# The second half's mixer: projection blocks in another order, convolution steps spread out, scores from split operands

## The chip, the cores and the metric

The kernel runs on one core of one Trainium2 chip. The metric is the device time of one execution in microseconds (us); lower is better. Engines are named as in the profile: PE (TensorE matmul), PEld (its weight load), DVE (VectorE), ACT (ScalarE), POOL (GpSimd), SP (SyncE, which here only starts the weight transfers).

## What is computed

The reference chains two blocks of two layers each, on 256 positions of width 1024, in float32. The change is in the mixer of the second block, which runs once per layer, so twice. Cut to that mixer:

```python
u = rms_norm_2(h, norm_mix[i])
q, k, v, c, g = jnp.split(u @ w_in[i], splits, axis=-1)      # 512, 128, 128, 1024, 2048 columns
q = rms_norm_2(q.reshape(B, S, N_HEADS, HEAD_DIM), q_norm[i])      # 8 heads of 64
k = rms_norm_2(k.reshape(B, S, KV_HEADS, HEAD_DIM), k_norm[i])     # 2 heads of 64
y_attn = window_attention(q, k, v, sink[i], rel_bias) @ w_attn_out[i]   # scores, bias, sink, softmax
c_val, c_gate = jnp.split(c, 2, axis=-1)
c = c_val * jax.nn.sigmoid(c_gate)
c = depthwise_conv(c, conv_w[i], conv_b[i])                  # 31 taps, 512 channels
c = jax.nn.silu(layer_norm_2(c, conv_ln_g[i], conv_ln_b[i]))
y_conv = c @ w_conv_out[i]
g_attn, g_conv = jnp.split(jax.nn.sigmoid(g), 2, axis=-1)
h = h + (g_attn * y_attn + g_conv * y_conv) @ w_o[i]
```

## The kernel before, in words

**Weights.** All weight matrices are one stream of blocks of 128x2048 floats. SP's queue brings block n into one of four slots of `raw` once PE has finished block n-4 (`blk_done`). ACT copies it, rounded, to `whi` (`split_hi`, L472), and DVE writes the rest, raw minus whi, to `wlo` (`split_lo`, L1094). Both do so two blocks ahead of PE (`AHEAD = 2`). PE then forms each product in float32 accuracy from three one-pass matmuls on rounded parts: hi by hi, hi by lo, lo by hi (`mm3`, L1973). A block of two 128x256 outputs is 48 matmuls.

**Every engine runs its own program in written order** and meets the others only at semaphores. Nothing is reordered at run time; what stands ahead of an instruction on its engine delays it. A DVE `split_lo(n)` waits for ACT's `split_hi(n)`, and PE's block n waits for `split_lo(n)`.

**The mixer (`window(l)` on ACT, DVE and PE).** It takes 16 such blocks, G to G+15: three for queries and keys (`sc` 16 to 21), one for values (`t_block`, evacuated by ACT), then the convolution's value and gate blocks in turn (four: value to `prod`, gate to `gated`, ACT's Sigmoid, product to `cpad`), then eight blocks of gates g. Blocks alternate between two PSUM banks of `ab`; `scaled_evac` (L1504, DVE) empties one with the factor of the RMS norm. `step()` is `split_lo(g+2)` and on to the next block.

**Norm of queries and keys.** ACT squares the six tiles (L941); PE sums them over the heads (`wvar_ps`, six matmuls in full float32, L2496); ACT takes Ln (L958) and Exp (L963), which gives `wstd_ready`; DVE scales the six tiles (L1814), which gives `wqk_ready`. PE's first scores wait for that.

**Attention.** `attend(i)` does three stages for three heads: scores of head i (L2371: one float32 matmul over the head's 64 rows, and two one-pass matmuls that add the position bias from `hank`; all of it twice, for two blocks of 128 queries), transposes of head i-1 (L2380, after `p_norm`, the normalised weights from ACT L827), and the product with the values of head i-2 (L2399, after `pt_ready`). DVE takes the maximum (`top`, L1651, L1655), ACT the Exp (L836), DVE the reciprocal of the sum (`normal`). PE runs one block G+5 to G+14 ahead of each of attend(0) to attend(9). Block G+15 follows attend(9).

**Convolution.** 31 taps on four channel groups of 128x256 are 124 DVE instructions per layer (L1780 for the first tap, L1784 for the rest), which `TAP_PLAN` spreads over ten steps, 12 or 14 instructions each. At the end DVE adds the four groups (L1794, L1795: `conv_ready`), PE takes the mean (L2514), and the convolution's layer norm follows; PE meanwhile does the first block of the attention's output projection, and waits in its middle for the variance (L2519).

Of the kernel before, what the change touches and what calls it, by code (L numbers as in the profile page):

```python
# [18 lines left out]
F32 = mybir.dt.float32  # L19
# [7 lines left out]
P = 128  # L27
# [65 lines left out]
def build(nc, xT, xn, lnrows, gaterows, stream, start, mods, params, wbd, wa2, pT, pos, masks, onehot, rb, toep, outT):  # L93
    with ExitStack() as ctx:
# [360 lines left out]
        def _(act):  # L455
# [473 lines left out]
            def window(l):  # L929
# [5 lines left out]
                for _ in range(3):  # L935
                    split_hi(g[0] + AHEAD)
                    tick()

                split_hi(g[0] + AHEAD)
                act.wait_ge(bank_evac[(a[0] - 1) % 2], (a[0] - 1) // 2 + 1)  # L940
                nc.scalar.activation(sc[:, 32:38, :], sc[:, 16:22, :], ACT.Square).then_inc(wsq_ready, 1)  # L941
                act.wait_ge(rcol_ps, l + 1)
                nc.scalar.activation(small[:, 8:10], mb[:, 0, 0:2], ACT.Copy).then_inc(rcol_ready, 1)
# [6 lines left out]
                tick()  # L950

                for j in range(12):
                    split_hi(g[0] + AHEAD)
                    if j == 0:
                        act.wait_ge(wvar_ps, l + 1)
                        for i in range(3):
                            bank = [mb[:, 0, :], mb[:, 1, :], acc[:, 0, :]][i]
                            ins = nc.scalar.activation(sc[:, 32 + 2 * i:34 + 2 * i, :], v2(bank), ACT.Ln,  # L958
                                                       bias=col("eps6"))
                        ins.then_inc(wln_ready, 1)  # L960
                        act.wait_ge(wln_ready, l + 1)

                        nc.scalar.activation(sc[:, 32:38, :], sc[:, 32:38, :], ACT.Exp, scale=-0.5)\  # L963
                            .then_inc(wstd_ready, 1)
                    elif j in (1, 3):
                        act.wait_ge(bank_evac[a[0] % 2], a[0] // 2 + 1)
                        nc.scalar.activation(gated, gated, ACT.Sigmoid).then_inc(csig_ready, 1)
                    tick()
                    if j >= 1:
                        attend(8 + 8 * l, j - 1, 1.0, l)  # L970
# [1758 lines left out]
```

## Time and profile before

| | |
|---|---|
| time, median of 3 runs | 2356.0 us (2355.74 to 2357.81) |
| the profiled execution's own time | 2353.87 us |
| its span, first to last instruction | 2352.1 us |
| PE busy | 2242.0 us, 95% |
| DVE busy | 1765.5 us, 75% |
| ACT busy | 1192.8 us, 51% |
| mean granted TensorE clock | 0.992 of full speed |
| share of the chain that ended last, by engine | PE 78%, DVE 12%, ACT 5%, DMA 3%, issue 2% |

The two mixers' 16 blocks stand at 1354 to 1484 us and at 1947 to 2080 us of the span. The rows further down are from the timeline (start, duration, engine, line, operation, written<-read, count, and in brackets the idle time of the engine before it and who ended it) and from a table of stretches.

### The profile page before, as it was taken

What the parts mean: (1) busy time and instruction counts of PE and PEld (TensorE: products, weight loads), DVE (VectorE), ACT (ScalarE), POOL (GpSimd) and SP (SyncE); (2) the same over time, 40 slices, a digit from 0 to 9 for tenths busy, and PEclk for the clock granted to TensorE, in tenths of its full rate; (3) what the DMA queues carried; (4) which work ended last, traced back from release to release, by engine and by line L of the source; (5) the groups of instructions that cost most, each with busy time, mean ns of one, the idle gap of its engine ahead of it and who ended that gap; (6) DMA issues with size and microseconds to landing.
All of it is one profiled execution on the core that took longest, in us unless ns stands there. A gap on an engine that the chain in (4) does not pass through costs nothing.

```text
span 2352.1 us, 36839 instructions
## 1 busy us (share of the span) xinstructions
PE 2242.0 (95%) x14676; PEld 2026.0 (86%) x14676; DVE 1765.5 (75%) x1857; ACT 1192.8 (51%) x1297; POOL 237.0 (10%) x199
## 2 busy tenths in 40 slices
PE   4999889999999998999999999999999999999999
PEld 4998789788889877788788998988998899798899
DVE  5898786788789985867667569877567746997755
ACT  2444555455455445555455455655455535565544
POOL 0113000001101300000022000012002200001200
PEclk9999999999999999999999999999999999999999
DMA  8996433567669852455555443445545554245553
GB/s 347 346 361 243 168 131 126 206 251 283 247 233 359 315 212 83 176 190 215 187 179 186 171 161 108 162 180 191 183 167 179 191 183 162 93 157 181 187 188 130
DMA packets 75934, 471.48 MB, mean 200 GB/s; under 512 B 8707, under 2 KB 8963, under 8 KB 27580
## 3 DMA queue, kind: packets, MB, share of 16 engines
q1 hardware_dynamic: 53136, 383.80, 44.7%
q0 software_dynamic: 18976, 68.71, 7.8%
q10 hardware_dynamic: 3724, 17.56, 2.0%
q8 instruction: 74, 1.21, 0.2%
q14 instruction: 24, 0.20, 0.0%
HBM read 468.97 MB, written 1.06 MB: 200 GB/s over the span
## 4 chain that ended last, share of the span: by engine, by line
PE 78%; DVE 12%; ACT 5%; DMA 3%; issue 2%; ACTq 0%; DVEq 0%; SPq 0%
PE ab L1973 18%; PE acc L1973 13%; PE acc L2114 12%; PE mb L2006 10%; PE ab L2006 9%; PE mb L2008 5%; PE ab L2008 5%; DVE wlo L1094 3%; ACT whi L472 2%; PE mb L2371 1%; DMA modmem<-mods 1%; DMA par<-params 1%; DMA raw<-stream 1%; DVE sc L1784 1%; DVE sc L1233 1%
## 5 line engine op out<-in xcount | busy, mean ns | idle before, releaser
L1094 DVE TENSOR_TENSOR wlo<-raw,whi 128x2048 fp32r<-128x2048 f32 x361 | 831.8, 2307 | 247.7 <-ACT whi L472 245.0
L472 ACT ACTIVATE whi<-raw 128x2048 fp32r<-128x2048 f32 x361 | 689.2, 1911 | 395.9 <-DMA raw<-stream 272.5
L1973 PE MATMUL ab<-uu,whi 128*128 128x256 f32 x3104 | 575.3, 288 | 20.4 <-DVE wlo L1094 9.3
L1973 PEld LDWEIGHTS ab<-uu,whi 128*128 128x128 f32 x3104 | 491.7, 195 | 32.0 <-issue 17.2
L1973 PE MATMUL ab<-uu,wlo 128*128 128x256 f32 x1552 | 443.2, 286 | 0.0
L2006 PE MATMUL ab<-uu,whi 128*128 128x512 f32 x1056 | 377.0, 400 | 8.4 <-DVE uu L1445 5.4
L2006 PE MATMUL mb<-uu,whi 128*128 128x512 f32 x1056 | 377.7, 400 | 3.2 <-DVE wlo L1094 1.8
L1973 PEld LDWEIGHTS ab<-uu,wlo 128*128 128x128 f32 x1552 | 302.1, 195 | 0.0
L1973 PE MATMUL acc<-h_hi,whi 128*128 128x256 f32 (+1 forms) x1032 | 293.7, 285 | 6.6 <-DVE h_lo L1721 2.6
L2008 PE MATMUL ab<-uu,wlo 128*128 128x256 f32 x1056 | 296.8, 281 | 0.0
L2008 PE MATMUL mb<-uu,wlo 128*128 128x256 f32 x1056 | 296.7, 281 | 0.0
L1973 PE MATMUL acc<-h_lo,whi 128*128 128x256 f32 (+1 forms) x1032 | 292.3, 283 | 0.0
L1973 PE MATMUL acc<-h_hi,wlo 128*128 128x256 f32 (+1 forms) x1032 | 292.3, 283 | 0.0
L2006 PEld LDWEIGHTS ab<-uu,whi 128*128 128x128 f32 x1056 | 199.1, 189 | 59.1 <-issue 8.6
L2006 PEld LDWEIGHTS mb<-uu,whi 128*128 128x128 f32 x1056 | 199.1, 189 | 54.7 <-DVE wlo L1094 3.3
L446 POOL TENSOR_TENSOR sc<-sc,rstd 128x512 f32<-128x512 f32 x44 | 120.0, 2727 | 964.4 <-ACT sc L691 964.4
L1973 PEld LDWEIGHTS acc<-h_hi,whi 128*128 128x128 f32 x1032 | 198.1, 192 | 8.4 <-DVE h_lo L1721 3.0
L2008 PEld LDWEIGHTS mb<-uu,wlo 128*128 128x128 f32 x1056 | 200.2, 190 | 0.1
L2008 PEld LDWEIGHTS ab<-uu,wlo 128*128 128x128 f32 x1056 | 200.2, 190 | 0.0
L1973 PEld LDWEIGHTS acc<-h_lo,whi 128*128 128x128 f32 x1032 | 198.2, 192 | 0.1
L1973 PEld LDWEIGHTS acc<-h_hi,wlo 128*128 128x128 f32 x1032 | 198.2, 192 | 0.0
L427 POOL DMA_DIRECT2D modmem<-mods x128 | 68.2, 533 | 947.4 <-DVE sc L1230 668.4
(352 smaller groups left out, 2817.1 us busy)
## 6 DMA issues: line engine op xcount, KB each, us to landing
raw<-stream SPq DMA_DIRECT2D x365, 1024.0 KB, 4.8
modmem<-mods POOLq DMA_DIRECT2D x128, 512.0 KB, 6.0
sc<-lnrows ACTq DMA_DIRECT2D x5, 1024.0 KB, 4.9
sc<-start ACTq DMA_DIRECT2D x4, 1024.0 KB, 16.5
gateb<-gaterows ACTq DMA_DIRECT2D x6, 512.0 KB, 3.7
hank<-toep POOLq DMA_DIRECT2D x8, 192.0 KB, 4.2
x<-xT ACTq DMA_DIRECT2D x1, 1024.0 KB, 31.4
x<-xn ACTq DMA_DIRECT2D x1, 1024.0 KB, 5.0
```

The lines of the kernel that those rows point to most:

```text
L427: pool.dma_start(modmem[:, i % MODRING, :], mods[i]).then_inc(mod_in[i % MODRING], 16)
L446: nc.gpsimd.tensor_tensor(gated, gated, r, ALU.mult).then_inc(g2_ready, 1)
L472: nc.scalar.activation(whi[:, n % RAW, :], raw[:, n % RAW, :], ACT.Copy).then_inc(hi_ready, 1)
L1094: nc.vector.tensor_tensor(wlo[:, n % RAW, :], raw[:, n % RAW, :], whi[:, n % RAW, :].bitcast(F32), ALU.subtract).then_inc(lo_ready, 1)
L1233: nc.vector.scalar_tensor_tensor(out=out, in0=part, scalar=cact[:, k:k + 1], in1=out, op0=ALU.mult, op1=ALU.add).then_inc(mod_done, 1)
L1784: ins = nc.vector.scalar_tensor_tensor(out=sc[:, 28 + c, :], in0=cpad[:, c, t:t + T], scalar=w, in1=sc[:, 28 + c, :], op0=ALU.mult, op1=AL ...
L1973: ins = nc.tensor.matmul(out, l, r, start=first and i == 0, stop=last and i == 2, skip_group_check=True)
L2006: nc.tensor.matmul(bank[:, m, :].rearrange("p (a t) -> p a t", a=2), wh[:, k, m * P:m * P + P], uu[:, :, k, :], start=k == 0, stop=k == DM ...
L2008: ins = nc.tensor.matmul(bank[:, m, 0:T], wl[:, k, m * P:m * P + P], u_hi[:, k, :], start=False, stop=k == DM - 1, skip_group_check=True)
L2114: ins = nc.tensor.matmul(acc[:, 2 * t + c, :], l, w[:, k, 512 * c:512 * c + 512], start=first and k == 0 and w is wh and l is hh, stop=las ...
L2371: ins = nc.tensor.matmul(mb[:, k % 2, o:o + w], l, r, start=(c == 0), stop=(c == len(terms) - 1), skip_group_check=True)
```

## The change

What it does, on ACT, DVE and PE alike:

- **Order of the 16 blocks.** Before: q, q, k, values, conv value 0, conv gate 0, conv value 1, conv gate 1, then eight gates. Now: conv value 0, conv gate 0, q, q, k, conv value 1, conv gate 1, values, then eight gates. `lay_out` writes the stream in the new order.
- **Attention's places.** attend(0) now follows block G+6 and attend(1) follows the values' block G+7; attend(2) to attend(9) follow G+8 to G+15. So attend(9) follows the last block, where before it stood one block ahead.
- **The sums of squares** (`variances`) stand between the two halves of block G+5, the second conv value block; before, they followed a whole conv value block.
- **Scores.** The one float32 matmul becomes three one-pass matmuls on rounded parts. So ACT writes the scaled queries' and keys' rounded part to `h_hi` (four instructions per layer, in two groups), and DVE the rest to `h_lo` (four instructions per layer, in two groups, between its scaling instructions). attend(0) waits for the first group, attend(2) for the second.
- **Taps** are spread over 15 steps, beginning after block G+1. The counts are pairs of instructions: 2, 3, 3, 2, 3, 2, 4, 5, 7, 6, 6, 6, 6, 4, 3.

```diff
+TAP_PLAN = {1: (0, 0, 2), 2: (0, 2, 3), 3: (0, 5, 3), 4: (0, 8, 2), 5: (0, 10, 3), 6: (0, 13, 2), 7: (0, 15, 4),
...
@@ ACT, window
+                act.wait_ge(bank_evac[a[0] % 2], a[0] // 2 + 1)
+                nc.scalar.activation(sc[:, 32:38, :], sc[:, 16:22, :], ACT.Square).then_inc(wsq_ready, 1)
+                tick()
+
+                act.wait_ge(wvar_ps, l + 1)
...
+                act.wait_ge(wln_ready, l + 1)
+                nc.scalar.activation(sc[:, 32:38, :], sc[:, 32:38, :], ACT.Exp, scale=-0.5).then_inc(wstd_ready, 1)
+                split_hi(g[0] + AHEAD)
+                act.wait_ge(cn_ready, 2 + 2 * l + 1)
+                for i in (0, 4):
+                    ins = nc.scalar.activation(h_hi[:, 16 + i, :], sc[:, 16 + i, :], ACT.Copy)
+                ins.then_inc(cnhi_ready, 1)
...
@@ DVE, window
+                scaled_evac(prod)
+                step()
+                taps(*TAP_PLAN[5])
+                link(nc.vector.tensor_scalar(small[:, 0:1], col("q_norm_2", l), 64.0 ** -0.5, None, ALU.mult))
+                dve.wait_ge(wstd_ready, l + 1)
+                scale_qk((0, 4)).then_inc(cn_ready, 1)
+                scale_qk((1, 2))
+                dve.wait_ge(cnhi_ready, 2 + 2 * l + 1)
+                rest_qk(((0, 1), (4, 1))).then_inc(wqk_ready, 1)
+                scale_qk((3, 5)).then_inc(cn_ready, 1)
+                scaled_evac(gated)
+                dve.wait_ge(cnhi_ready, 2 + 2 * l + 2)
+                rest_qk(((1, 3), (5, 1))).then_inc(wqk_ready, 1)
+                step()
+                top(n, 0, 1.0, l)
+                conv_in(2)
+                taps(*TAP_PLAN[6])
+                normal(n, 0, l)
+                step()
...
@@ PE, window
+                a_block(g[0], a[0], None, (0, 1), variances)
+                g[0] += 1
+                a[0] += 1
+                a_static(1)
...
-                    return [(sc[r, 16 + h // 2, qb * P:qb * P + P], sc[r, 20 + h // 4, :], 0, T),
+                    qs, ks = slice(qb * P, qb * P + P), 20 + h // 4
+                    return [(h_hi[r, 16 + h // 2, qs], h_hi[r, ks, :], 0, T),
+                            (h_lo[r, 16 + h // 2, qs], h_hi[r, ks, :], 0, T),
+                            (h_hi[r, 16 + h // 2, qs], h_lo[r, ks, :], 0, T),
                             (flip[:], hank_hi[:, h, P * (1 - qb):P * (1 - qb) + T], 0, T),
...
+                pe.wait_ge(wqk_ready, 2 + 2 * l + 1)
+                pe.wait_ge(hanklo_ready, 1)
+                attend(8 + 8 * l, 0, qk, lambda h, kt: vw[:, kt, 64 * (h // 4):64 * (h // 4) + 64], l)
+                v_an = a[0]
+                t_block(P)
+                attend(8 + 8 * l, 1, qk, lambda h, kt: vw[:, kt, 64 * (h // 4):64 * (h // 4) + 64], l)
```

**Place 1, ACT, around the norm of queries and keys.** The rows name line, operation, written<-read and the semaphores waited for; line numbers of the changed kernel differ. Before:

```order
L472 ACTIVATE whi<-raw 128x2048 [waits raw_ready2]
L958 ACT_TABLE_LOAD
L958 ACTIVATE sc<-mb,par 128x512 [waits wvar_ps]
L958 ACTIVATE sc<-mb,par 128x512
L958 ACTIVATE sc<-acc,par 128x512
L963 ACT_TABLE_LOAD
L963 ACTIVATE sc<-sc 128x1536 [waits wln_ready]
L472 ACTIVATE whi<-raw 128x2048 [waits raw_ready3]
L967 ACT_TABLE_LOAD
L967 ACTIVATE sc<-sc 128x512 [waits bank_evac1]
```

Now:

```order
L470 ACTIVATE whi<-raw 128x2048 [waits raw_ready2]
L948 ACTIVATE small<-mb 128x2 [waits rcol_ps]
L950 ACTIVATE sc<-sc 128x1536 [waits bank_evac0]
L956 ACT_TABLE_LOAD
L956 ACTIVATE sc<-mb,par 128x512 [waits wvar_ps]
L956 ACTIVATE sc<-mb,par 128x512
L956 ACTIVATE sc<-acc,par 128x512
L959 ACT_TABLE_LOAD
L959 ACTIVATE sc<-sc 128x1536 [waits wln_ready]
L470 ACTIVATE whi<-raw 128x2048 [waits raw_ready3]
L963 ACTIVATE h_hi<-sc 128x256 [waits cn_ready]
L963 ACTIVATE h_hi<-sc 128x256
```

The weight copy behind the Exp is that of block G+7 before and now. What moved is the copy of block G+6, which now stands ahead of the Square (first row), and the first group of ACT's new copies to `h_hi`, which stands behind the copy of G+7.

**Place 2, DVE, from the evacuation ahead of the scaling to the one behind it.** Before (block G+4's evacuation, the lo part of G+6, the scaling):

```order
L1504 TENSOR_TENSOR sc<-ab,rstd 128x512 [waits blk_done]
L1094 TENSOR_TENSOR wlo_49<-raw,whi 128x2048 [waits hi_ready]
L1811 TENSOR_SCALAR small<-par 128x1 [waits wstd_ready]
L1814 SCALAR_TENSOR_TENSOR sc<-sc,small 128x256 [waits dve_chain]
L1814 SCALAR_TENSOR_TENSOR sc<-sc,small 128x256 x3
L1814 SCALAR_TENSOR_TENSOR sc<-sc,par 128x256 x2
L1504 TENSOR_TENSOR sc<-ab,rstd 128x512 [waits blk_done]
L1094 TENSOR_TENSOR wlo_49<-raw,whi 128x2048 [waits hi_ready]
L1819 TENSOR_TENSOR sc<-sc 128x2x256 [waits csig_ready]
```

Now (block G+5's evacuation, the lo part of G+7, six tap instructions, the scaling, and block G+6's evacuation):

```order
L1523 TENSOR_TENSOR sc<-ab,rstd 128x512 [waits blk_done]
L1113 TENSOR_TENSOR wlo_49<-raw,whi 128x2048 [waits hi_ready]
L1801 SCALAR_TENSOR_TENSOR sc<-sc,par 128x256 [waits tap_done] x6
L1838 TENSOR_SCALAR small<-par 128x1
L1816 SCALAR_TENSOR_TENSOR sc<-sc,small 128x256 [waits wstd_ready,dve_chain]
L1816 SCALAR_TENSOR_TENSOR sc<-sc,par 128x256
L1816 SCALAR_TENSOR_TENSOR sc<-sc,small 128x256 x2
L1823 TENSOR_TENSOR h_lo<-sc,h_hi 128x256 [waits cnhi_ready]
L1823 TENSOR_TENSOR h_lo<-sc,h_hi 128x256
L1816 SCALAR_TENSOR_TENSOR sc<-sc,small 128x256
L1816 SCALAR_TENSOR_TENSOR sc<-sc,par 128x256
L1523 TENSOR_TENSOR sc<-ab,rstd 128x512 [waits blk_done]
```

Before, the lo part of G+7 stood behind the scaling; now it stands ahead of it, and waits for `hi_ready` of block G+7. Six tap instructions stand ahead of the scaling too; between the scaling instructions stand the new subtractions to `h_lo`.

**Place 3, the mixer's end.** DVE before:

```order
L1784 SCALAR_TENSOR_TENSOR sc<-sc,par 128x256 [waits tap_done] x6
L1686 TENSOR_TENSOR h_lo<-acc,h_hi 128x256 [waits ohi_ready]
L1794 TENSOR_TENSOR sc<-sc 128x512 [waits tap_done]
L1795 TENSOR_TENSOR sc<-sc 128x256 [waits dve_chain]
L1094 TENSOR_TENSOR wlo_49<-raw,whi 128x2048 [waits hi_ready]
L1504 TENSOR_TENSOR sc<-ab,rstd 128x512 [waits blk_done]
L1834 SCALAR_TENSOR_TENSOR sc<-mb,sc 128x1024 [waits cmean_ps]
```

DVE now:

```order
L1801 SCALAR_TENSOR_TENSOR sc<-sc,par 128x256 [waits tap_done] x14
L1705 TENSOR_TENSOR h_lo<-acc,h_hi 128x256 [waits ohi_ready]
L1872 TENSOR_TENSOR sc<-sc 128x512 [waits tap_done]
L1873 TENSOR_TENSOR sc<-sc 128x256 [waits dve_chain]
L1113 TENSOR_TENSOR wlo_49<-raw,whi 128x2048 [waits hi_ready]
L1523 TENSOR_TENSOR sc<-ab,rstd 128x512 [waits blk_done]
L1881 SCALAR_TENSOR_TENSOR sc<-mb,sc 128x1024 [waits cmean_ps]
```

PE before, the last matmuls of block G+15 and what follows:

```order
L1973 MATMUL ab<-uu,whi 128x256 x2
L1973 MATMUL ab<-uu,wlo_49 128x256
L1973 MATMUL ab<-uu,whi 128x256 x2
L1973 MATMUL ab<-uu,wlo_49 128x256
L2514 MATMUL mb<-sc,mean_r_53 128x256 [waits conv_ready]
L1973 MATMUL acc<-h_hi,whi 128x256 [waits lo_ready,olo_ready]
```

PE now:

```order
L2020 MATMUL ab<-uu,whi 128x256 x2
L2020 MATMUL ab<-uu,wlo_49 128x256
L2448 MATMUL acc<-sc 64x256 [waits olo_ready,pt_ready]
L2448 MATMUL acc<-sc 64x256
L2579 MATMUL mb<-sc,mean_r_53 128x256 [waits conv_ready]
L2020 MATMUL acc<-h_hi,whi 128x256 [waits lo_ready,olo_ready]
```

On DVE the rows are the same but for the number of taps; on PE the product with the last head's values (attend(9)) now stands between the last block and the mean, where the whole block G+15 stood between them before.

## Rows read from the trace of the kernel before

**Rows 1.** The page: the chain that ended last, by engine, shares of the span.

```profile
PE 78%; DVE 12%; ACT 5%; DMA 3%; issue 2%; ACTq 0%; DVEq 0%; SPq 0%
```

**Rows 2.** Timeline of PE, one steady step of the first mixer.

```profile
1416.52 0.51 PE L1973 MATMUL ab<-uu,whi 128*128 128x256 f32 x2
...
1422.47 0.70 PE L2371 MATMUL mb<-sc 64*128 64x256 f32 x2
1423.09 0.38 PE L2371 MATMUL mb<-hank_hi,flip 128*128 128x256 f32 x1
...
1424.49 0.60 PE L2380 MATMUL acc<-par,sc 128*128 128x128 f32 x4
...
1426.03 0.51 PE L1973 MATMUL ab<-uu,whi 128*128 128x256 f32 x2
```

**Rows 3.** Timeline of PE, the first mixer from the values' block to head 0's transposes.

```profile
1372.43 0.30 PE L1973 MATMUL ab<-whi,uu 128*128 128x128 f32 x1
...
1383.63 0.81 PE L2496 MATMUL mb<-sc,par 128*128 128x256 f32 x3
...
1386.03 0.58 PE L1973 MATMUL ab<-uu,whi 128*128 128x256 f32 x2
...
1393.81 0.70 PE L2371 MATMUL mb<-sc 64*128 64x256 f32 x2 [1.68 <-DVE sc L1814]
...
1403.16 0.70 PE L2371 MATMUL mb<-sc 64*128 64x256 f32 x2
...
1414.93 0.55 PE L2380 MATMUL acc<-par,sc 128*128 128x128 f32 x3 [1.29 <-ACT sc L827]
```

**Rows 4.** Timeline of PE, the second mixer.

```profile
1986.73 0.48 PE L2371 MATMUL mb<-sc 64*128 64x256 f32 x1 [1.68 <-DVE sc L1814]
...
2007.51 0.90 PE L2380 MATMUL acc<-par,sc 128*128 128x128 f32 x3 [2.43 <-ACT sc L827]
...
2017.76 0.48 PE L2371 MATMUL mb<-sc 64*128 64x256 f32 x1
```

**Rows 5.** Stretches: from:to, length, busy time by engine, clock, DMA.

```profile
1397.00:1399.00 2.00, 2.00 (x11) 2.00 (x11) 1.93 (x6) 0.82 (x3) 0.00 (x0) 0.50 0.00 0
2010.40:2012.00 1.60, 1.60 (x8) 1.55 (x8) 1.60 (x5) 1.60 (x5) 0.00 (x0) 0.50 0.00 0
```

**Rows 6.** Timeline of ACT, the first mixer.

```profile
1386.42 1.27 ACT L958 ACTIVATE sc<-mb,par 128x512 f32<-128x512 f32 x2 [4.61 <-PE acc L2496]
...
1389.58 1.49 ACT L963 ACTIVATE sc<-sc 128x1536 f32<-128x1536 f32 x1
1390.97 1.90 ACT L472 ACTIVATE whi<-raw 128x2048 fp32r<-128x2048 f32 x1
...
1417.24 0.47 ACT L836 ACTIVATE sc<-mb,small 128x256 f32<-128x256 f32 x1 [1.06 <-DVE small L1655]
...
1420.62 0.90 ACT L827 ACTIVATE sc<-sc,small 128x256 f32<-128x256 f32 x2
...
1478.49 0.39 ACT L859 ACTIVATE h_hi<-acc 128x256 fp32r<-128x256 f32 x1 [2.32 <-PE acc L2399]
```

**Rows 7.** Timeline of DVE, a steady step and the mixer's end.

```profile
1423.52 2.29 DVE L1094 TENSOR_TENSOR wlo<-raw,whi 128x2048 fp32r<-128x2048 f32 x1
1425.72 0.69 DVE L1651 TENSOR_REDUCE small<-mb 128x2 f32<-128x512 f32 x1
...
1426.58 2.46 DVE L1784 SCALAR_TENSOR_TENSOR sc<-sc,par 128x256 f32<-128x256 f32 x6
...
1433.31 2.29 DVE L1094 TENSOR_TENSOR wlo<-raw,whi 128x2048 fp32r<-128x2048 f32 x1
...
1482.66 0.42 DVE L1686 TENSOR_TENSOR h_lo<-acc,h_hi 128x256 fp32r<-128x256 f32 x1
```

**Rows 8.** Timeline of PE, the end of the first mixer.

```profile
1477.38 0.86 PE L2399 MATMUL acc<-sc 128*64 128x256 f32 x3
...
1484.23 0.45 PE L2514 MATMUL mb<-sc,mean_r 128*128 128x256 f32 x1
```

More of the change, by code:

```diff
@@ L933, in tick, with sigmoid @@
                     g[0] += 1
-                for _ in range(3):
+                def sigmoid(i):
+                    act.wait_ge(bank_evac[a[0] % 2], a[0] // 2 + 1)
+                    nc.scalar.activation(gated, gated, ACT.Sigmoid).then_inc(csig_ready, 1)
+                split_hi(g[0] + AHEAD)
+                tick()
+                split_hi(g[0] + AHEAD)
+                sigmoid(0)
+                tick()
+                for _ in range(2):
                     split_hi(g[0] + AHEAD)
@@ L950, in window @@
                 tick()
-                for j in range(12):
+                attend(8 + 8 * l, 1, 1.0, l)
+                for i in range(2, 10):
                     split_hi(g[0] + AHEAD)
[L954 to L967, printed above, removed]
                     tick()
-                    if j >= 1:
-                        attend(8 + 8 * l, j - 1, 1.0, l)
-                    if j == 9:
-                        b = a[0] - 3
+                    attend(8 + 8 * l, i, 1.0, l)
+                    if i == 8:
+                        b = a[0] - 4
                         act.wait_ge(bank_evac[b % 2], b // 2 + 1)
@@ L1763, in window @@
             def window(l):
-                for i in range(3):
-                    scaled_evac(sc[:, 16 + 2 * i:18 + 2 * i, :])
-                    step()
+                scaled_evac(prod)
                 step()
@@ new lines, in window @@
+                scaled_evac(gated)
+                dve.wait_ge(cnhi_ready, 2 + 2 * l + 2)
+                rest_qk(((1, 3), (5, 1))).then_inc(wqk_ready, 1)
+                step()
+                top(n, 0, 1.0, l)
+                conv_in(2)
+                taps(*TAP_PLAN[6])
+                normal(n, 0, l)
+                step()
+                top(n, 1, 1.0, l)
+                taps(*TAP_PLAN[7])
+                normal(n, 1, l)
+                for i in range(2, 10):
+                    if i < 9:
+                        scaled_evac(sc[:, 2 * (i - 2):2 * (i - 2) + 2, :])
+                        step()
+                    pair, first, count = TAP_PLAN[6 + i]
+                    if i < 8:
+                        top(n, i, 1.0, l)
+                        taps(pair, first, count // 2)
+                        normal(n, i, l)
+                        taps(pair, first + count // 2, count - count // 2)
+                    else:
+                        taps(pair, first, count)
+                    rest(n, i - 2, l)
+                    if i == 9:
@@ L1978, in split_ready, with a_block @@
                 pe.wait_ge(lo_ready, at(n + 1, it))
-            def a_block(n, an, it=None, ms=(0, 1)):
+            def a_block(n, an, it=None, ms=(0, 1), between=None):
                 split_ready(n, it)
@@ L1987, in a_block @@
                 for m in ms:
+                    if between is not None and m == 1:
+                        between()
                     for k in range(DM):
```

111 lines of the change are left out of this document (56 added, 55 removed).

## The prediction

> **What bounds the kernel now.** I read the chain that ended last first: PE holds 78% of it, DVE 12%, ACT 5% [rows 1]. So work that leaves DVE or ACT gains nothing by itself; what counts is PE's own time and the moments at which PE stands still. Then I walked PE's timeline through the two mixers. A steady step of attention (block, scores, transposes, values' product) repeats every 9.51 us, from 1416.52 to 1426.03, with no idle time in brackets [rows 2]: block 5.95, scores 2.02 (1422.47 to 1424.49), the rest 1.54. DVE's step in that place, from one weight split to the next, is 9.79 us with fourteen tap instructions [rows 7], so PE and DVE are nearly even, and PE is the one that never waits.
>
> PE stands still at two places per mixer ahead of that. In the first mixer it waits 1.68 us for the scaled queries and keys and 1.29 us for the first head's normalised weights [rows 3]; in the second 1.68 and 2.43 us [rows 4]. And the clock falls behind some waits: in the first mixer, scores plus block take 9.35 us (1393.81 to 1403.16) [rows 3] where the steady ones take 7.97 [rows 2], a loss of 1.38; the granted clock is 0.50, the 1.2 GHz level, from 1397 to 1399 [rows 5]. In the second, transposes to the next scores take 10.25 us (2007.51 to 2017.76) [rows 4] against 7.49 (1424.49 to 1431.98, one 9.51 step later than 1422.47) [rows 2], a loss of 2.76 at 0.50 again [rows 5]. All this together is what the change could remove: 1.68 + 1.38 + 1.29 = 4.35 in the first, 1.68 + 2.43 + 2.76 = 6.87 in the second, **11.2 us**.
>
> **One-pass scores.** Removed are 32 float32 matmuls (8 heads, 2 query blocks, 2 layers), added are 96 one-pass ones. The float32 one holds PE for 0.62 us until the bias matmul (1422.47 to 1423.09) [rows 2]. The six float32 matmuls of the sums of squares, over all 128 rows, take 2.40 us, 0.40 each (1383.63 to 1386.03) [rows 3]. The difference of about 0.2 is a pause between the 64-row and the 128-row matmuls, not the passes. A one-pass matmul costs 0.12 (48 of them and a start in 5.95) [rows 2], so three cost 0.36. If the pause stays: 0.62 - (0.36 + 0.2) = 0.06 or 0.07 each, times 32, **2.2 us gained**. I take that, since the new matmuls are 64-row ones as well. Ends: if the pause belonged to float32 and goes, 0.26 each, 8.4 us gained; if each of the three cost 0.22 instead, like the spacing of a lone matmul after a pause, 0.66 against 0.62, some 1 us lost.
>
> The Trainium skill, TensorEngine Tiling (Array Packing), Key Properties, says that a change of tiling mode, not only of tile, drains TensorE. By that rule the pause stays and the gain is 2.2 us; without it, 8.4. The 0.2 us seen here agree with it.
>
> **The wait ahead of attend(0), followed instruction by instruction.** Let zero be the start of the six sums of squares. PE is then free for the scores after 2.40 of sums, the second half of block G+5 (2.9), and block G+6 (5.85): at 11.2. Does the Square come in time? It has half a block, 2.9 us, for an evacuation and the Square; I cost that at nothing, with about half a us to spare.
>
> ACT: Ln starts at 2.79 (1386.42 less 1383.63), Exp at 5.95, and the weight copy of G+7 runs from 7.34 to 9.24 [rows 3, 6]. Before, DVE scaled right behind the Exp. Now DVE has first to write the lo part of G+7, which needs that very copy; so DVE, idle since it emptied block G+5, starts it at 9.3 and takes 2.2 (1423.52 to 1425.72) [rows 7]: 11.5. Six tap instructions, 2.4 [rows 7]: 13.9. The small factor and two scaling instructions, 1.05 at 0.4 each like a tap: 14.95. ACT's two copies of 128x256, 0.39 each [rows 6], overlapping: 15.65. DVE's two subtractions at 0.42 and some overlap (the h_lo row) [rows 7]: 16.4. PE resumes at 16.4 instead of 11.2: **a wait of 5.2 us**, in place of 1.68. Queued behind it on PE are all scores, and behind the split on DVE the evacuation of G+6, which nobody misses for two blocks.
>
> **The wait ahead of the first transposes.** After 16.4 DVE does two scalings, waits for ACT's 128x768 and 128x256 copies, evacuates, subtracts (to 19.7, by the same per-element times), then needs ACT's copy of G+8 (to 20.2), splits (22.4) and takes the maximum (0.86) [rows 7]: 23.3, with ACT's Sigmoid beside it. From the Exp of a head to the end of the next normalisation ACT needs 4.28 (1417.24 to 1420.62 and 0.90) [rows 6], here with the values' evacuation in place of the transposes' copy: 27.6. PE is there after scores 1.95, values' block 5.35 (1372.43 to 1383.63 less a block of 5.85) [rows 3] and scores 1.95: 25.7. **A wait of 1.9 us** if the clock holds. It won't: it fell for a wait of 2.43 and for one of the two of 1.68, so I expect it for 5.2. Then PE loses up to 2.76 as in the second mixer and arrives at 28.5, past 27.6, so the two don't add: 5.2 + 2.8 = **8.0 us** for both waits and the clock, against 7.1 at full clock.
>
> **The mixer's end.** Before, block G+15 hid head 7's last steps: product at 1477.38, mean at 1484.23 with no wait [rows 8]. Now the mean comes right behind the product. ACT's rounded part starts 1.11 us after the product (1478.49 less 1477.38) [rows 6, 8] and takes 0.39; DVE's lo part and the two additions of the taps lead to the mean 1.57 us after the lo part's start (1482.66 to 1484.23) [rows 7, 8]. So the mean starts 3.1 after the product, which itself needs 1.0: **2.1 us of new wait**. The wait for the variance that follows has the same chain as before and stays. 2.1 lies between the waits that did and didn't lower the clock; the variance wait would swallow half of a drop of 2.8, so I add half of 1.4, 0.7.
>
> **The steady steps.** PE's step goes from 9.51 to 9.37. DVE's is 9.79 with fourteen tap instructions; with twelve, 9.0 [rows 7]. One step has fourteen still, and DVE enters the row with 2 to 3 us in hand, so DVE doesn't bind. The taps moved into the first steps run while DVE idled; I cost them at nothing but for the six ahead of the scaling, counted above. The eight new instructions on ACT and DVE, about 2 us on each per layer, are hidden but for those in the chain. The new stream order moves no transfer to another time.
>
> **Sum.** Removed: 11.2 + 2.2 = 13.4. Added per mixer: 8.0 + 2.1 + 0.7 = 10.8, twice 21.6. Net **+8.2 us**. On the profiled execution's own 2353.87 that is 2362.1; that execution lies 2.1 below the median of the runs, 2356.0, so the median comes to **2364 us**, 0.35% slower. A measurement of this kernel can tell about 0.2%, 4.7 us, from no change.
>
> **Rivals.**
> - *The scaling isn't late.* If DVE got the lo part of G+7 without waiting for ACT (scaling ends with the Exp's chain at 13.3 instead of 16.4), the first wait is 2.1 and the clock mostly holds: per mixer 2.1 + 1.9 + 2.1 = 6.1, twice 12.2, less 13.4: 2355 us, no change. If even that wait vanished (everything done by 11.2), 2 x (1.9 + 2.1) = 8.0 less 13.4: **2350.6 us, faster**. It decides from a scaling chain that ends by 11.2. Against it stand the order of DVE's and ACT's instructions and the 9.24 at which the copy ends; for it only that my zero may be off.
> - *The pause was float32's.* The scores gain 8.4, the net is +2.0: 2358 us, the same. PE's step would fall to 9.0, where DVE's 9.0 begins to bind, so little more can come of it. Against: the pause is as long ahead of the bias matmul as 64 against 128 rows would make it.
> - *The clock stays low longer* after 5.2 us than after 2.43, or falls at the end as well: up to 2 us more per mixer, 2368 us.
> - *The change doesn't spread DVE's work*: with DVE binding in the steps of six taps, 9.8 against 9.37 for five steps, 2 us per mixer more: 2368 us as well.
>
> **Chances.** Forecast with its clock variants, slower by over 0.2%: 0.60 (2364, of which 0.15 for the two rivals at 2368). The same: 0.26 (2355 to 2360: half-late scaling 0.13, cheaper pause 0.13). Faster: 0.14, the scaling in time. The range reaches from 2354 to 2369: it leaves out the 2350.6 and a little above the clock's worst, and takes in the scores' ends.
>
> **What would show it.** In the trace after: a wait of about 5 us of PE at the first scores of each mixer, ended by DVE's h_lo; the clock at 0.50 behind it; DVE idle for 3 us ahead of the lo part of G+7, ended by ACT's copy; a wait of 2.1 us at the mean; score groups of 1.9 us and steps of 9.4. Score groups of 1.5 us would refute the pause, and a first wait under 2 us the whole forecast.

## Result, and the profile of the changed kernel

The changed kernel takes 2368.32 us, the median of four runs (2366.73 to 2371.21), the kernel before 2355.87 in four runs on the same chip (2353.01 to 2357.81): 1.0063 times as long, 95% interval 1.0046 to 1.0080. The profiled execution took 2367.62 us with a span of 2365.7, against 2353.87 and 2352.1 before.

The chain that ended last, by engine, answers [rows 1]: PE's share rose from 78 to 82%.

```profile
PE 82%; DVE 9%; ACT 5%; DMA 2%; issue 1%; ACTq 0%; DVEq 0%; SPq 0%
```

PE's timeline at the first mixer answers [rows 3] and [rows 2]. Columns: start, busy us, engine, line, operation, written<-read, shapes, count, and in brackets the idle time ahead and what ended it. First the sums of squares, then each place's first row.

```profile
1386.64 1.89 PE L2547 MATMUL mb<-sc,par 128*128 128x256 f32 x8
...
1403.16 0.58 PE L2420 MATMUL mb<-h_hi 64*128 64x256 f32 x1 [5.14 <-DVE h_lo L1823]
...
1406.35 0.31 PE L2020 MATMUL ab<-whi,uu 128*128 128x128 f32 x1
...
1416.61 0.58 PE L2420 MATMUL mb<-h_hi 64*128 64x256 f32 x1
...
1420.51 0.78 PE L2020 MATMUL ab<-uu,whi 128*128 128x256 f32 x2
...
1427.49 0.38 PE L2420 MATMUL mb<-h_hi 64*128 64x256 f32 x1
...
1429.37 0.60 PE L2429 MATMUL acc<-par,sc 128*128 128x128 f32 x4
...
1430.90 0.39 PE L2020 MATMUL ab<-uu,whi 128*128 128x256 f32 x1
...
1436.85 0.38 PE L2420 MATMUL mb<-h_hi 64*128 64x256 f32 x1
```

There is one wait up to here, 5.14 us, where the kernel before had 1.68 and 1.29; in the second mixer it is 5.15. PE doesn't wait again before the mixer's end, but everything behind the wait is slow: scores 3.19 us (1403.16 to 1406.35), the values' block 10.26 (to 1416.61), scores 3.19, then block G+8 6.98 (1420.51 to 1427.49). From 1427.49 on the pace is that of a steady step: scores 1.88, and 9.36 from one step's scores to the next (1427.49 to 1436.85).

The stretches of that time, with the granted clock ahead of the DMA share (columns: stretch, length, busy time of PE, its weight loads, DVE, ACT and POOL, granted clock, DMA share, GB/s), answer [rows 5]:

```profile
1403.10:1406.30 3.20, 3.14 (x10) 2.47 (x11) 2.59 (x6) 2.37 (x3) 0.00 (x0) 0.50 0.02 5
1406.40:1416.30 9.90, 9.90 (x49) 9.90 (x48) 7.92 (x12) 6.68 (x10) 0.00 (x0) 0.50 0.00 1
1416.60:1419.80 3.20, 3.20 (x11) 2.52 (x11) 0.00 (x0) 1.42 (x4) 0.00 (x0) 0.50 0.60 169
1422.00:1423.00 1.00, 1.00 (x7) 1.00 (x7) 1.00 (x4) 1.00 (x4) 0.00 (x0) 0.54 0.00 0
1423.00:1424.00 1.00, 1.00 (x10) 1.00 (x10) 1.00 (x3) 1.00 (x1) 0.00 (x0) 1.00 0.00 0
1494.10:1497.00 2.90, 2.90 (x14) 2.85 (x15) 2.90 (x3) 0.20 (x1) 0.00 (x0) 0.59 0.41 172
```

PE was busy all the time from 1403.16 to 1423, and the clock was at 1.2 GHz (0.50) for nearly all of it, 19.8 us (19.3 in the second mixer). It rose at 1422.9, 2.4 us into block G+8. In the kernel before, the clock's falls cost 1.38 and 2.76 us.

Who made PE wait, on DVE (answers [rows 7]):

```profile
1395.91 2.29 DVE L1113 TENSOR_TENSOR wlo<-raw,whi 128x2048 fp32r<-128x2048 f32 x1 [2.92 <-ACT whi L470]
1398.12 2.46 DVE L1801 SCALAR_TENSOR_TENSOR sc<-sc,par 128x256 f32<-128x256 f32 x6
...
1400.68 0.48 DVE L1816 SCALAR_TENSOR_TENSOR sc<-sc,small 128x256 f32<-128x256 f32 x1
...
1402.35 0.76 DVE L1823 TENSOR_TENSOR h_lo<-sc,h_hi 128x256 fp32r<-128x256 f32 x2
```

DVE idles 2.92 us until ACT has rounded block G+7, writes its lo part, does six tap instructions, and only then scales. The mixer's end, on PE, answers [rows 8]; first the variance's row in the kernel before, then the changed kernel's rows:

```profile
1490.40 0.70 PE L2519 MATMUL mb<-sc,mean_r 128*128 128x256 f32 x2 [1.21 <-DVE sc L1838]
```

```profile
1491.00 1.08 PE L2448 MATMUL acc<-sc 128*64 128x256 f32 x4
1494.07 0.74 PE L2579 MATMUL mb<-sc,mean_r 128*128 128x256 f32 x2 [1.99 <-DVE sc L1873]
...
1500.40 0.59 PE L2584 MATMUL mb<-sc,mean_r 128*128 128x256 f32 x2
```

The mean waits 1.99 us and starts 3.07 after the product; behind it the clock is low once more (0.59 until 1497), and the variance comes 6.33 us after the mean with no wait, where it took 6.17 with a wait of 1.21 before (1484.23 to 1490.40).

### The profile page after: what moved, and what is told of

Same layout as the page of the kernel before. It is cut to its first block, busy times and chain, and to the rows that moved or that the text cites. A ratio compares the mean times of both kernels' runs of the same rounds, so it can differ in the third digit from the quotient of the medians.

```text
span 2365.7 us, 36919 instructions
## 1 busy us (share of the span) xinstructions
PE 2256.9 (95%) x14708; PEld 2050.0 (87%) x14708; DVE 1770.3 (75%) x1865; ACT 1194.3 (50%) x1303; POOL 236.8 (10%) x199
## 3 DMA queue, kind: packets, MB, share of 16 engines
q8 instruction: 74, 1.21, 0.2%
## 4 chain that ended last, share of the span: by engine, by line
PE 82%; DVE 9%; ACT 5%; DMA 2%; issue 1%; ACTq 0%; DVEq 0%; SPq 0%
PE ab L2020 21%; PE acc L2020 13%; PE acc L2163 12%; PE mb L2055 10%; PE ab L2055 10%; PE mb L2057 5%; PE ab L2057 5%; DVE wlo L1113 3%; PE mb L2420 2%; ACT whi L470 2%; DMA par<-params 1%; DMA raw<-stream 1%; PE acc L2448 1%; PE mb L2020 0%; DVE sc L1252 0%
```

## The experiments

The question after the result was what the clock's part hangs on, since the waits at the first scores and at the mean had come as computed. **Theory A**: the length of the wait sets how long the clock stays low. **Theory B**: what PE does behind the wait sets it; in the changed kernel that is scores, the values' block (48 matmuls of 128 columns, where other blocks have 256), and scores. These runs are on several chips, so each kernel is compared by its ratio to the kernel before on the same chip, which took 2351 to 2353 us there. All are edits of the changed kernel but the one that names the kernel before. Rows and stretches are of one profiled execution each.

**The changed kernel again.**

> The changed kernel itself, for a time on the same chip as the other runs of this row: 2366 to 2370 us, 1.0063 times the kernel before.

2368.53 us, ratio 1.0064 (1.0040 to 1.0088). The result repeats: the waits are the same 5.14 us, and the low clock behind them lasted 20.5 and 18.6 us.

**ACT's rounding of G+7 early.**

```diff
@@ ACT, window
                 tick()
+                split_hi(g[0] + AHEAD)
 
                 act.wait_ge(wvar_ps, l + 1)
...
                 nc.scalar.activation(sc[:, 32:38, :], sc[:, 32:38, :], ACT.Exp, scale=-0.5).then_inc(wstd_ready, 1)
-                split_hi(g[0] + AHEAD)
```

> The changed kernel with one move: ACT rounds the weights of block G+7 ahead of the logarithms, not behind the exponential. Theory A (DVE's split of G+7, queued ahead of the scaling, waits for ACT's rounding, and the length of PE's wait sets how long the clock stays low): from the start of the sums of squares, the rounding ends at 1.9, the split at 8.3, six taps at 10.7, the scaling's chain at 13.2, against PE's 11.2: a wait of about 2.0 us in place of 5.15, with 3 us or less lost to the clock behind it in place of 8.2; per mixer some 8 us less, near 2352 us. Rival B (what PE does behind the wait, the scores and the values' block of 128 columns, sets how long the clock stays low): the same wait of 2.0, but 0.50 for 19 us again, only 3.1 us per mixer less, 2362 us. Rival C (DVE is late for another reason): the wait stays at 5 us and the time at 2368.

2364.66 us, ratio 1.0046 (1.0031 to 1.0062). The wait shrank to 2.13 us, so DVE did wait for ACT's rounding. PE's timeline, the first rows of scores, values' block, block G+8 and scores:

```profile
1401.76 0.38 PE L2420 MATMUL mb<-h_hi 64*128 64x256 f32 x1 [2.13 <-DVE h_lo L1823]
...
1403.64 0.22 PE L2020 MATMUL ab<-whi,uu 128*128 128x128 f32 x1
...
1417.68 0.78 PE L2020 MATMUL ab<-uu,whi 128*128 128x256 f32 x2
...
1424.99 0.38 PE L2420 MATMUL mb<-h_hi 64*128 64x256 f32 x1
```

The stretch in which the clock rose:

```profile
1420.00:1421.00 1.00, 1.00 (x7) 1.00 (x7) 1.00 (x4) 1.00 (x1) 0.00 (x0) 0.58 0.00 0
```

The first scores still ran at full pace (1.88 us), but the clock was at 0.50 right behind them, from about 1403.8 to 1420.8, 17 us (20 in the second mixer), and block G+8 took 7.31 us. From the first scores to the end of block G+8 it is 23.23 us, where the changed kernel has 24.33 and a kernel without waits (below) 15.43: the wait fell by 3.0 us, the clock's part only from 8.9 to 7.8. That is rival B, which had 2362 us.

**A longer wait in the kernel before.** Two subtractions that nobody uses, ahead of the scaling.

```diff
@@ DVE, window, kernel before
                         dve.wait_ge(wstd_ready, l + 1)
+                        link(nc.vector.tensor_tensor(sc[:, 0:8, :], sc[:, 8:16, :], sc[:, 8:16, :], ALU.subtract))
+                        link(nc.vector.tensor_tensor(sc[:, 0:5, :], sc[:, 8:13, :], sc[:, 8:13, :], ALU.subtract))
```

> The kernel before with work added that is used by nobody: two subtractions, 128x2048 and 128x1280, on DVE ahead of the scaling, 3.6 us. PE's wait at the first scores becomes 5.2 to 5.4 us in place of 1.68, with scores, a full block of 256 columns and scores behind it. Theory A (the length of the wait sets the clock's fall): 0.50 for about 19 us as in the changed kernel, 3.6 us and 6 to 8 us more per mixer, less the 1.3 to 2.4 us of the second wait that a low clock swallows: 2371 to 2376 us. Rival B (what follows sets it): 0.50 for some 3 to 6 us as in the kernel before: 3.6 us per mixer and at most 2 for the clock: 2363 to 2367 us.

2362.84 us, ratio 1.0051 (1.0034 to 1.0068). PE's rows of scores, a full block, and scores, then the stretches:

```profile
1394.64 1.22 PE L2373 MATMUL mb<-sc 64*128 64x256 f32 x2 [5.54 <-DVE sc L1816]
...
1398.25 0.63 PE L1975 MATMUL ab<-uu,whi 128*128 128x256 f32 x2
...
1405.81 0.70 PE L2373 MATMUL mb<-sc 64*128 64x256 f32 x2
```

```profile
1394.70:1398.20 3.50, 3.50 (x8) 1.98 (x9) 3.29 (x3) 1.91 (x2) 0.00 (x0) 0.50 0.00 0
...
1402.00:1403.00 1.00, 1.00 (x10) 1.00 (x9) 1.00 (x4) 1.00 (x3) 0.00 (x0) 0.91 0.00 0
```

A wait even longer than the changed kernel's, with a full block behind its scores, was followed by 7.5 us of low clock (8.6 in the second mixer), not 20. Theory A falls. The time is at the lower edge of what B gives, 2363 to 2367.

**The values' block in 256 columns.** The 128 more columns are padding.

```diff
@@ PE, window
-                t_block(P)
+                t_block(T)
```

> The changed kernel with the values' block computed in 256 columns in place of 128; the 128 more are padding that nobody reads. PE's work grows by some 0.5 us per mixer at full clock (48 matmuls at 0.12 for 0.11). The wait of 5.15 us and everything else stay. Theory B (what PE does behind the wait sets how long the clock stays low, as the runs with the earlier rounding and with a longer wait in the kernel before suggest): 0.50 for some 4 to 7 us in place of 19, so 4 to 6 us less per mixer, part of it taken back by the wait at the first transposes: 2358 to 2362 us. Theory A (the length of the wait sets it): 0.50 for 19 us again, 2368 to 2370 us.

2359.43 us, ratio 1.0032 (1.0017 to 1.0047): 9 us less than the changed kernel on the same chip, with more work. The wait is the same. The time is in B's range. The first rows of scores, values' block, scores, and the scores behind block G+8; then the stretch in which the clock rose:

```profile
1401.65 0.53 PE L2420 MATMUL mb<-h_hi 64*128 64x256 f32 x1 [5.15 <-DVE h_lo L1823]
...
1404.79 0.41 PE L2020 MATMUL ab<-whi,uu 128*128 128x256 f32 x1
...
1412.28 0.38 PE L2420 MATMUL mb<-h_hi 64*128 64x256 f32 x1
...
1420.44 0.38 PE L2420 MATMUL mb<-h_hi 64*128 64x256 f32 x1
```

```profile
1408.00:1409.00 1.00, 1.00 (x8) 1.00 (x8) 0.96 (x3) 0.99 (x2) 0.00 (x0) 0.72 0.00 0
```

The block of twice the columns took 7.49 us in place of 10.26, since the clock rose in the middle of it, after 7 us in place of 20 (5.5 in place of 19 in the second mixer). This shows B directly, for the values' block: nothing but its columns was changed. No run here changes the scores behind the wait in number or rows, so what they contribute isn't shown.

**Both moves together.** The two diffs above, in one kernel.

> Both single moves together: ACT's rounding of G+7 ahead of the logarithms, and the values' block in 256 columns, half of which is padding that nobody reads. The wait at the first scores is then 2.1 us, as with the rounding alone. Theory B (what stands behind the wait sets how long the clock stays low): 0.50 for 3 to 6 us, not for the 17 of the same wait with 128 columns; from 2366 to 2353 to 2356 us on a chip where the kernel before takes 2352. If the columns had nothing to do with it: 17 us low again, 2362.

2351.69 us, ratio 0.9999 (0.9987 to 1.0011). The wait is 2.13 us, and the clock is back at 1.00 in the stretch from 1408 on, having fallen at about 1401.2: under 7 us. The time is 1.3 us under the lower end of what B gave, 2353 to 2356.

```profile
1401.20:1402.70 1.50, 1.50 (x6) 1.28 (x6) 0.88 (x2) 1.50 (x3) 0.00 (x0) 0.50 0.83 344
...
1408.00:1409.00 1.00, 1.00 (x11) 1.00 (x10) 1.00 (x4) 1.00 (x4) 0.00 (x0) 1.00 0.02 8
```

So the low stretch in the first mixer is 20 and 17 us with 128 columns (waits of 5.14 and 2.13), and 7 and under 7 with 256 (waits of 5.15 and 2.13). Over both mixers of all the kernels in which the values' block of 128 columns follows the first wait, two of them further down, it is 17 to 23 us.

**The scaling early too.** The early rounding, and on DVE:

```diff
@@ DVE, window
                 scaled_evac(prod)
-                step()
-                taps(*TAP_PLAN[5])
...
                 scale_qk((3, 5)).then_inc(cn_ready, 1)
+                step()
+                taps(*TAP_PLAN[5])
                 scaled_evac(gated)
```

> The same, and DVE does the scaling of queries and keys ahead of the split of G+7 and of the six taps. All theories: no wait at the first scores (the chain ends at about 9.5, PE comes at 11.2), and one at the first transposes, where the first head's maximum now stands behind the taps and the split of G+8: about 4 us (24.4 against 20.4 from the start of the sums of squares). Theory A (the length of the wait sets the clock's fall): 4 us and some 6 us lost to the clock per mixer in place of 5.2 and 8.2, near 2362 us. Rival B (what follows sets it; here a product, then full blocks of 256 columns): 4 us and 3 at most for the clock, near 2355 us.

2352.20 us, ratio 1.0000 (0.9986 to 1.0013). No wait at the first scores, the values' block at full clock (5.40 us), and a new wait at the first transposes:

```profile
1415.80 1.11 PE L2429 MATMUL acc<-par,sc 128*128 128x128 f32 x4 [4.00 <-ACT sc L825]
1416.57 0.78 PE L2020 MATMUL ab<-uu,whi 128*128 128x256 f32 x2
...
1424.24 0.38 PE L2420 MATMUL mb<-h_hi 64*128 64x256 f32 x1
```

The wait of 4.00 is as computed, and the block behind it takes 7.67 us for 5.95: 1.7 us for the clock. B had 2355 us for this kernel, A 2362. (The profiled execution, 2359.76 us, was the slowest of the ten.) Without a wait ahead of it, the values' block of 128 columns ran at the full clock; behind a wait the clock stayed low through all of it.

**Float32 scores.** The one-pass scores undone; roundings and lo parts are still made.

```diff
@@ PE, qk of window
-                    return [(h_hi[r, 16 + h // 2, qs], h_hi[r, ks, :], 0, T),
-                            (h_lo[r, 16 + h // 2, qs], h_hi[r, ks, :], 0, T),
-                            (h_hi[r, 16 + h // 2, qs], h_lo[r, ks, :], 0, T),
+                    return [(sc[r, 16 + h // 2, qs], sc[r, ks, :], 0, T),
```

> The changed kernel with one part undone: the scores' products in float32 from the unrounded queries and keys, one matmul in place of three; the roundings and lo parts are still made and waited for. If three one-pass matmuls take what a float32 one does less 0.14 per head (0.06 to 0.07 per product): the steady step goes from 9.36 back to 9.51 us, 2.2 us more in all, near 2368 to 2370 us. If the pause belonged to float32, 8 us more.

2375.07 us, ratio 1.0088 (1.0063 to 1.0112), above the 2368 to 2370 us expected. Between 1428.07 and 1437.57 a step takes 9.50 us in place of 9.36:

```profile
1428.07 0.70 PE L2420 MATMUL mb<-sc 64*128 64x256 f32 x2
...
1437.57 0.70 PE L2420 MATMUL mb<-sc 64*128 64x256 f32 x2
```

That is 0.14 per head, 2.2 us in all, the prediction's term. The medians differ by 6.5 us, with intervals of some 5.7 us to each side, and at the low clock a group of float32 scores takes 3.61 us (1394.64 to 1398.25 in the kernel with the longer wait) where the one-pass group takes 3.19, twice per mixer. From the one-column products (L2536, one block and a half ahead of the sums of squares) to the mean its two mixers take 117.76 and 119.12 us, against 116.51 and 116.32: 4.1 us together, with the low clock 3 us longer in the second. So the median alone doesn't tell 2.2 from 8; the step does, and the rest of the 6.5 us is not explained.

**The convolution's sums ahead of the last lo part.**

```diff
@@ DVE, window, i == 9
-                    rest(n, i - 2, l)
+                    if i < 9:
+                        rest(n, i - 2, l)
...
                         nc.vector.tensor_tensor(sc[:, 32, :], sc[:, 32, :], sc[:, 33, :], ALU.add).then_inc(conv_ready, 1)
+                        rest(n, 7, l)
@@ PE, window
-                pe.wait_ge(olo_ready, 8 + 4 * l + 4)
+                pe.wait_ge(olo_ready, 8 + 4 * l + 3)
...
                 def variance():
+                    pe.wait_ge(olo_ready, 8 + 4 * l + 4)
```

> The changed kernel with the two additions of the convolution's sums ahead of the last pair's lo part on DVE; PE needs that lo part only for the fourth pair of output tiles. The chain from the last product to the mean loses ACT's rounding and DVE's subtraction: a wait at the mean of about 1.0 us in place of 1.99. If the mechanism is right: 1 us less per mixer, 2366 us, and up to 1.5 us more per mixer if the clock no longer falls there (2363). Rival (the taps end too late for it to matter): the wait stays near 2 us, and the time at 2368.

2368.95 us, ratio 1.0083 (1.0062 to 1.0104): nothing gained.

```profile
1492.40 0.70 PE L2582 MATMUL mb<-sc,mean_r 128*128 128x256 f32 x2 [1.32 <-DVE sc L1875]
1499.03 0.67 PE L2588 MATMUL mb<-sc,mean_r 128*128 128x256 f32 x2 [1.63 <-DVE sc L1888]
```

The mean's wait fell to 1.32, with the fourteen tap instructions ahead of the sums now the last to end, and 1.63 us of wait came up at the variance, whose chain goes through DVE: a weight split stands there ahead of the centring. From the last product to the variance it is 9.03 us in place of 9.40. The 1 us per mixer that was expected left that split out.

**All waits taken out, first try.** The early rounding and scaling; the first head's maximum ahead of the second lo parts, its weights on ACT ahead of the rounding of G+9; the second sigmoid and `conv_in(2)` at a later head; the sums right behind the taps; and another tap table:

```diff
-TAP_PLAN = {1: (0, 0, 2), 2: (0, 2, 3), 3: (0, 5, 3), 4: (0, 8, 2), 5: (0, 10, 3), 6: (0, 13, 2), 7: (0, 15, 4),
-            8: (0, 19, 5), 9: (0, 24, 7), 10: (1, 0, 6), 11: (1, 6, 6), 12: (1, 12, 6), 13: (1, 18, 6), 14: (1, 24, 4), 15: (1, 28, 3)}
+TAP_PLAN = {1: (0, 0, 3), 2: (0, 3, 3), 3: (0, 6, 3), 4: (0, 9, 6), 5: (0, 15, 1), 6: (0, 16, 4), 7: (0, 20, 5),
+            8: (0, 25, 6), 9: (1, 0, 6), 10: (1, 6, 5), 11: (1, 11, 6), 12: (1, 17, 5), 13: (1, 22, 5), 14: (1, 27, 3), 15: (1, 30, 1)}
@@ DVE, window
                 scaled_evac(gated)
+                top(n, 0, 1.0, l)
                 dve.wait_ge(cnhi_ready, 2 + 2 * l + 2)
                 rest_qk(((1, 3), (5, 1))).then_inc(wqk_ready, 1)
+                normal(n, 0, l)
                 step()
```

> From the kernel with the early rounding and the early scaling: the first head's maximum goes ahead of the second lo parts and of the split of G+8, its weights are normalised on ACT ahead of the rounding of G+9, the second sigmoid and convolution input move to the third head, the taps are spread so that six of 31 steps stand in DVE's idle time at the sums of squares and one is left at the end, the convolution's sums go right behind them, and ACT's last rounding and the gate's sigmoid stand ahead of the last pair. The theory that waits and what stands behind them make the whole loss: no wait at the first scores, the first transposes and the mean, no low clock, 6 us less per mixer than with the wait of 4.0 at the transposes and 2 to 3 less at the end: 2334 to 2338 us, against 2351 for the kernel before on this chip. Rival (DVE's order only hands the wait on, to a weight split or to the variance): a new wait of 1 to 3 us per mixer, 2340 to 2348 us.

2345.25 us, ratio 0.9968 (0.9953 to 0.9982): faster than the changed kernel and the one before, but at 2340 to 2348 us, as the rival had it: waits were only handed on. PE's waits that were left, at the second head's transposes and at the variance (in the second mixer 2.91 us), and on ACT what delays the variance's chain:

```profile
1411.32 1.12 PE L2439 MATMUL acc<-par,sc 128*128 128x128 f32 x4 [1.72 <-ACT sc L821]
...
1482.92 0.67 PE L2595 MATMUL mb<-sc,mean_r 128*128 128x256 f32 x2 [1.17 <-DVE sc L1895]
```

```profile
1473.50 1.92 ACT L470 ACTIVATE whi<-raw 128x2048 fp32r<-128x2048 f32 x1 [2.19 <-DMA raw<-stream]
1475.43 1.28 ACT L995 ACT_TABLE_LOAD   x1
1476.73 1.92 ACT L995 ACTIVATE sc<-sc 128x2048 f32<-128x2048 f32 x1
1478.55 0.36 ACT L859 ACTIVATE h_hi<-acc 128x256 fp32r<-128x256 f32 x1
```

ACT waits 2.19 us for a transfer with a sigmoid behind it that could have run, and the last pair's rounding comes last.

**Second try.** The second head's weights' sum behind two tap steps; the sigmoid ahead of the rounding that waits for the transfer; the centring right behind the sums, the split behind the additions of the squares.

```diff
@@ DVE, window
-                taps(*TAP_PLAN[7])
+                pair, first, count = TAP_PLAN[7]
+                taps(pair, first, 2)
                 normal(n, 1, l)
+                taps(pair, first + 2, count - 2)
...
                 nc.vector.tensor_tensor(sc[:, 36, :], sc[:, 36, :], sc[:, 37, :], ALU.add).then_inc(csum_ready, 1)
+                split_lo(g[0] + AHEAD)
```

> The fastest kernel so far with three moves. Second head: its weights' sum is taken on DVE behind two of the tap steps and not behind all five, so the wait of 1.72 us at the second transposes, and the low clock behind it (about 1.5 us), go: 3 us per mixer. End: the centring on DVE stands right behind the convolution's sums, ahead of the last split and of the last pair's lo part, and ACT's gate sigmoid ahead of the rounding that waits for a transfer, so the waits at the variance (1.17 and 2.9 us) go. Theory: 10 us less, 2335 us. Rival (the split of G+17, now later, is waited for by the second half of the mixer's end, or the low clock falls elsewhere): 2340 to 2344 us.

2338.66 us, ratio 0.9945 (0.9931 to 0.9958), between theory and rival. The waits at the second head, the mean and the variance are gone; one of 1.34 us is left at the third head. On ACT a table load, the sigmoid of the second gate (0.63 us) and a rounding stand ahead of that head's weights; the second table load stands behind them:

```profile
1426.70 1.12 PE L2441 MATMUL acc<-par,sc 128*128 128x128 f32 x4 [1.34 <-ACT sc L821]
```

```profile
1422.12 1.28 ACT L1000 ACT_TABLE_LOAD   x1
...
1425.75 0.89 ACT L821 ACTIVATE sc<-sc,small 128x256 f32<-128x256 f32 x2
1426.66 1.28 ACT L836 ACT_TABLE_LOAD   x1
```

**Third try.** That sigmoid ahead of the exponential, where ACT idles.

```diff
@@ ACT, window, i == 2
-                    attend(8 + 8 * l, i, 1.0, l)
                     if i == 2:
+                        weights(9 + 8 * l)
                         b = a[0] - 3
                         act.wait_ge(bank_evac[b % 2], b // 2 + 1)
                         nc.scalar.activation(gated, gated, ACT.Sigmoid).then_inc(csig_ready, 1)
+                    attend(8 + 8 * l, i, 1.0, l)
```

> The fastest kernel so far with one move on ACT: the second sigmoid, with its two table loads, stands ahead of the third head's exponential, where ACT idles for 5.18 us, and not behind it. Theory (the sigmoid and its table load push the rounding of a block and with it the third head's weights past PE): the wait of 1.34 us at the third transposes goes, with 1.6 us of low clock behind it: 5 to 6 us less in all, near 2333 us against 2351 before. Rival (the weights are late because DVE's sum is): the wait stays, 2338 us.

**2333.70 us, ratio 0.9918** (0.9904 to 0.9932), on a chip where the kernel before takes 2352.11. PE has no wait in the mixers between the sums of squares and the variance, and the clock is 1.00 throughout; a stretch of 20 us in the attention:

```profile
1400.00:1420.00 20.00, 20.00 (x151) 18.00 (x151) 19.78 (x36) 13.54 (x23) 0.00 (x0) 1.00 0.45 159
```

DVE is busy 19.8 of 20 us there, nearly as full as PE, so another order can gain little more in this stretch.

## Why the prediction was right in direction and too low

**Right, by its steps.** The first wait: 5.2 us predicted, 5.14 and 5.15 measured, by the chain that was followed: ACT's rounding of G+7 at 1393.98, the split, six tap instructions, the scaling, the copies, the lo parts. The run with the early rounding, computed by the same steps at 2.0, gave 2.13. The second wait swallowed by the low clock: none is left, though both its ends came later than computed. The first head's weights were ready 31.6 us after the start of the sums of squares instead of 27.6, since ACT had to wait for the slow values' block, and PE was there at 33.2 instead of 28.5. The waits and losses of the kernel before, 11.2 us: gone. One-pass scores: a steady step of 9.36 against 9.37 predicted, a group of 1.88 to 1.90, and 0.14 per head in the run that undoes them. The pause between 64-row and 128-row matmuls stayed: the bias matmul starts 0.21 behind the last product's start (1427.83 to 1428.04), not 0.12. The Trainium skill, TensorEngine Tiling (Array Packing), Key Properties, has a change of tiling mode drain the engine; the 0.21 in place of 0.12 agrees with it. The mean's wait: 2.1 predicted, 1.99 measured. With the variance it came to 3.07 - 1.0 + 6.33 - 6.17 = 2.2 us per mixer, where 2.8 was added. DVE didn't bind: it idles up to 1.4 us a step, and PE doesn't wait there.

**Wrong: the price of the clock behind the first wait.** The step that failed is the clock's term in "5.2 + 2.8 = 8.0". The prediction took the loss of the second mixer before, 2.8 us, for the new wait: "Then PE loses up to 2.76 as in the second mixer". But there a full block of 256 columns stood behind the wait, and here scores, the values' block and scores. The five items from the first scores to the end of block G+8 take 24.33 us (1403.16 to 1427.49). In the first try without waits the same items take 15.43 (1392.13 to 1407.56), so the clock cost **8.9 us** in place of 2.8 (in the second mixer 24.15 against 15.43, 8.7). With the values' block widened and nothing else changed, the five items take 18.79 us (1401.65 to 1420.44): 5.5 of the missing 6 us come from what stood behind the wait. The wait and the clock make 14.0 where 8.0 were in the sum, 12 us too little over both mixers. The rival "the clock stays low longer" was the case, but priced at up to 2 us per mixer; it was 6. It was priced by what was seen before, not by what the change put behind the wait. The new order showed the values' block there, but no row of the kernel before has such a block behind a wait (there it ran at full clock), so its price couldn't be read, only left room for. That the rival's 2368 us meets the measured 2368.32 is luck: by the measured terms the sum is higher still.

**The sum with measured terms.** 8.2 + 2 x 6.0 - 2 x 0.6 = 19 us. In the traces, from the mixers' first block to behind the variance, the changed kernel takes 10.15 and 7.64 us longer, 17.8 together, so the terms hold where they were taken. The spans differ by 13.6, the medians by 12.4. The rest lies in stretches whose PE work is the same: between the mixers and behind the second one the changed kernel's execution is 2 us shorter each (462.2 against 460.2, and 266.4 against 264.3). From the first mixer's variance to the second's one-column products it took 478.3 us in one execution and 476.2 in another, and the first try 481.6. So a single execution tells a difference only to some us. The ratio's interval, 1.0046 to 1.0080, is 10.8 to 18.8 us: it holds 17.8 and 13.6, and the 19 lies at its edge.

Part of what varies there the traces show. Between the mixers, at 1754.83 in the kernel before, PE waits 2.1 us in every kernel. In 8 of the 13 profiled executions the clock fell within 2 us of that wait (in the first try from 1748.5 to 1755.3), in the kernel before and in both executions of the changed kernel it didn't. The 2 us by which stretches differ at full clock aren't explained.

The kernels that take the cause away confirm the account from the other side: with the waits out and one-pass scores in, 18 us less than before (2352.11 to 2333.70). The prediction's sum for that case is 2.2 of scores and 11.2 of waits and clock, 13.4; the waits at the variance, 1.21 and its like in the second mixer, make up 2.4 of the rest, and some 2.6 us stay open. The idea of the change was sound; its order on DVE and ACT wasn't.

## What to carry to other kernels

Price a wait on PE as the wait plus the low clock behind it, and read the second part from rows in which the same work stands behind a wait, not from another wait of the same kernel. Here the low clock lasted 3 to 9 us where scores and a block of 256 columns stood behind the wait, and 17 to 23 where scores and the values' block of 128 columns did. Where such a wait can't be avoided, try a wider block behind it, even one that computes padding: here that took 9 us off. When a dependent step moves, list what stands ahead of it on each engine it passes. Here the rounding that one weight split waited for made 3.0 of the 5.14 us of wait; but with it out of the way 7.8 of the 8.9 us of clock stayed, and only scaling ahead of the split and the taps took both away at the first scores.

## What the runs showed of the hardware

- With PE busy without a gap from 1403.16 on, the clock stayed at 1.2 GHz for 19.8 us in the changed kernel, and a block of twice the columns was the faster one: 7.49 against 10.26 us.
- At full clock the values' block, 48 matmuls of 128 columns, takes 5.40 us (1394.00 to 1399.40 in the first try), a block of 48 with 256 columns 5.95 (1430.90 to 1436.85): half the columns save almost nothing. At 1.2 GHz a matmul of either kind starts every 0.21 us.
- After the changed kernel's waits of 5.14 and 5.15 us the clock was low from the first matmul or, in the repeat, 0.1 us later; after one of 2.13 it was still 1.00 for 0.7 to 2.0 us and fell then. Behind one and the same wait of 2.1 us, between the mixers, it fell in 8 executions of 13.
- A table load on ACT takes 1.28 us; one, with its sigmoid of 0.63, stood ahead of a head's weights when PE waited 1.34 us for them. With both moved to where ACT idled, that wait was gone.
